# Order of the w_in column groups: attention's queries, keys and values first, retention's behind them

## The reference, cut to what matters

```python
h = rmsnorm(x, g_mix)
z = h @ w_in
aq, ak, av, rq, rk, rv, rg, ga, gb = jnp.split(z, SPLIT_POINTS, axis=-1)
aq = rope_half(aq.reshape(B, S, N_Q_HEADS, HEAD_DIM), pos)
ak = rope_half(ak.reshape(B, S, N_KV_HEADS, HEAD_DIM), pos)
ya = sliding_window_sink_attention(aq, ak, av, sinks) @ w_a
rq = retention_rotation(rq.reshape(B, S, RET_HEADS, RET_QK_DIM), pos)
rk = retention_rotation(rk.reshape(B, S, RET_HEADS, RET_QK_DIM), pos) * (RET_QK_DIM ** -0.5)
r = chunkwise_retention(rq, rk, rv)
r = r * lax.rsqrt(jnp.mean(r * r, axis=-1, keepdims=True) + EPS)
yb = (r.reshape(B, S, RET_V) * jax.nn.silu(rg)) @ w_b
x = x + (jax.nn.sigmoid(ga) * ya + jax.nn.sigmoid(gb) * yb) @ w_out
x = x + jnp.square(jax.nn.relu(rmsnorm(x, g_mlp) @ w_up)) @ w_down
```

## Time and profile before

| | before |
|---|---|
| runs shown | 1014.49, 1015.31, 1015.38 us, median 1015.31 us |
| the profiled execution | 1015.0 us, its span 1013.1 us |
| mean granted TensorE clock in it | 0.998 |
| busy: PE, DVE, ACT, POOL | 99%, 71%, 50%, 17% of the span |
| DMA, mean | 186 GB/s, 188.60 MB |

### The profile page before, as it was taken

The page is one execution under the profiler, slowest core; times in us unless marked ns, Lnnn a source line. Parts: engine busy times, 40 slices in busy tenths (PEclk is TensorE's granted clock), DMA queues, the critical chain, the costliest instruction groups (busy, mean ns, idle before and its releaser), DMA issues.

```text
span 1013.1 us, 13575 instructions
## 1 busy us (share of the span) xinstructions
PE 1004.5 (99%) x5653; PEld 850.0 (84%) x5653; DVE 720.8 (71%) x817; ACT 502.3 (50%) x616; POOL 170.7 (17%) x129
## 2 busy tenths in 40 slices
PE   9999999999999999999999999999999999999997
PEld 8887788888888888887788888888887899899796
DVE  5878656766565665787765667888877757789974
ACT  6544554454444545454554454444468545654352
POOL 0520000000000000430000020000000149169730
PEclk9999999999999999999999999999999999999999
DMA  9797444555556455596553557555554754345451
GB/s 341 250 288 246 160 155 142 170 180 191 199 176 207 166 178 175 187 294 225 166 167 125 169 147 283 201 177 209 204 170 135 238 178 167 125 166 141 121 188 41
DMA packets 103644, 188.60 MB, mean 186 GB/s; under 512 B 9160, under 2 KB 18464, under 8 KB 103456
## 3 DMA queue, kind: packets, MB, share of 16 engines
q1 hardware_dynamic: 103408, 187.66, 55.8%
q10 hardware_dynamic: 176, 0.09, 0.0%
HBM read 180.69 MB, written 4.72 MB: 183 GB/s over the span
## 4 chain that ended last, share of the span: by engine, by line
PE 93%; DVE 3%; DMA 1%; issue 1%; ACT 1%; SPq 0%; DVEq 0%; ACTq 0%
PE bank L786 13%; PE bank L789 12%; PE bank L788 12%; PE bank L1091 11%; PE bank L811 8%; PE bank L815 7%; PE bank L822 7%; PE bank L1095 6%; PE bank L1173 2%; DVE w_lo L1873 2%; PE bank L984 1%; PE bank L1397 1%; PE bank L968 1%; DMA a_bounce<-arena 1%; PE bank L793 1%; PE bank L803 1%
## 5 line engine op out<-in xcount | busy, mean ns | idle before, releaser
L1873 DVE TENSOR_TENSOR w_lo<-arena,w_hi 128x2048 fp32r<-128x2048 f32 (+1 forms) x80 | 185.1, 2323 | 95.2 <-ACT w_hi L1485 94.8
L1873 DVE TENSOR_TENSOR w_lo<-raw,w_hi 128x2048 fp32r<-128x2048 f32 (+1 forms) x78 | 181.1, 2331 | 80.1 <-ACT w_hi L1485 80.0
L1485 ACT ACTIVATE w_hi<-raw 128x2048 fp32r<-128x2048 f32 (+1 forms) x83 | 157.1, 1892 | 102.3 <-PE bank L789 71.4
L1485 ACT ACTIVATE w_hi<-arena 128x2048 fp32r<-128x2048 f32 (+1 forms) x80 | 151.3, 1892 | 104.6 <-PE bank L789 80.8
L1091 PE MATMUL bank<-hT,w_hi 128*128 128x512 f32 x504 | 123.4, 391 | 0.0
L786 PE MATMUL bank<-w_hi,hT 128*128 128x512 f32 (+1 forms) x296 | 114.1, 385 | 0.9 <-issue 0.9
L1091 PEld LDWEIGHTS bank<-hT,w_hi 128*128 128x128 f32 x504 | 92.2, 188 | 17.6
L2482 POOL TENSOR_TENSOR rstd<-mean,const 128x1 f32<-128x1 f32 (+1 forms) x16 | 9.1, 579 | 528.5 <-DVE mean L1882 359.4
L789 PE MATMUL bank<-w_hi,hT 128*128 128x512 f32 (+1 forms) x256 | 97.9, 382 | 0.0
L788 PE MATMUL bank<-w_lo,hT 128*128 128x512 f32 (+1 forms) x256 | 97.9, 382 | 0.0
L811 PE MATMUL bank<-w_hi,hT 128*128 128x512 f32 (+1 forms) x216 | 83.3, 388 | 0.7 <-DVE arena L2131 0.7
(11 more groups left out here) (342 smaller groups left out, 1886.7 us busy)
## 6 DMA issues: line engine op xcount, KB each, us to landing
arena<-in_w_in SPq DMA_DIRECT2D x22, 1024.0 KB, 5.3
raw<-in_w_in SPq DMA_DIRECT2D x20, 1024.0 KB, 5.3
arena<-in_w_up SPq DMA_DIRECT2D x16, 1024.0 KB, 5.3
raw<-in_w_up SPq DMA_DIRECT2D x16, 1024.0 KB, 5.3
arena<-in_w_down SPq DMA_DIRECT2D x16, 1024.0 KB, 5.1
raw<-in_w_down SPq DMA_DIRECT2D x16, 1024.0 KB, 5.1
raw<-in_e_w_in SPq DMA_DIRECT2D x6, 1024.0 KB, 5.1
arena<-in_e_w_in SPq DMA_DIRECT2D x6, 1024.0 KB, 5.1
```

The lines of the kernel that those rows point to most:

```text
L1485: act.activation(w_hi[:, p % SPLIT_RING, :, 0:n], raw_at(p)[:, :, 0:n], copy).then_inc(hi_ready, 1)
L1873: dve.tensor_tensor(w_lo[:, s, :, 0:n], raw_at(p)[:, :, 0:n], w_hi[:, s, :, 0:n].bitcast(F32), ALU.subtract).then_inc(lo_ready, 1)
```

## The change

The groups are numbered `AQ, AKV, RQ, RK, RV0, ...`. What depends on the numbers moves with them:

- the first group is AQ, the second the 256 columns of AKV, so that `second_group` is half as wide as before
- the tables att_cos and att_sin (64 KB) are loaded by themselves ahead of piece 3, the others ahead of piece 4 as before
- DVE runs `rotate_halves` in the window of g = 1 and `rotate_pairs` in that of g = 3, both with lo splits between; POOL runs them in that order too
- `turn_vectors` stands one group later on PE, and `spread_dt` on DVE behind the whole of `rotate_halves`
- SP stores attention's rows at piece 10 in one DMA (before: two, at 14 and 15) and fetches them at piece 11 in four (before eight, at 15); retention's rows are stored at 13 and fetched at 15 (before 12 and 13)
- DVE transposes aT at the start of g = 4 and rT at that of g = 6, each ahead of the next lo split (before rT at 5, aT at 6)
- attention's scores and softmax stand in the windows 4 to 7 (before 6 to 9), the transposes of probabilities in 5 to 8, the products with the values in 6 to 9 (bank 4, before 3); retention's scores in 6, 7 and 8 through bank 3 alone, its output in 8 and 9 (before 10 and 11 and behind), in the banks 6/7 and 2/5. No step stands behind the last group any more
- the second bank pair of the product with w_a waits for retention's output (`r_ready`), and DVE waits for `vec_ready` only ahead of the MLP

The core of the diff:

```diff
-RQ, RK, AQ, AKV, RV0, RV1, RG0, RG1, GA0, GA1, GB0, GB1 = range(12)
-W_IN_START = (768, 1280, 0, 512, 1792, 2304, 2816, 3328, 3840, 4352, 4864, 5376)
+AQ, AKV, RQ, RK, RV0, RV1, RG0, RG1, GA0, GA1, GB0, GB1 = range(12)
+W_IN_START = (0, 512, 768, 1280, 1792, 2304, 2816, 3328, 3840, 4352, 4864, 5376)
...
             def load(piece):
+                if n[0] == 3:
+                    sp.dma_start(const[:, FIRST_TABLES:SECOND_TABLES], consts[:, FIRST_TABLES:SECOND_TABLES]).then_inc(att_tables, 16)
...
             def blocks_moved(l, piece):
-                if piece == 12:
+                if piece == 10:
+                    for t in range(T):
+                        sp.wait_ge(rope_done[t], l + 1)
+                    store_rows(a_bounce.rearrange("(t p) n -> p t n", p=P), a_rows, a_stored)
+                if piece == 11:
+                    sp.wait_ge(a_stored, 16 * (l + 1))
+                    fetch_blocks(a_moved, a_bounce, a_blocks)
+                if piece == 13:
                     for t in range(T):
                         sp.wait_ge(rot_done[t], l + 1)
                     store_rows(r_bounce.rearrange("(t p) n -> p t n", p=P), z_ret, r_stored)
-                if piece == 13:
+                if piece == 15:
                     sp.wait_ge(r_stored, 16 * (l + 1))
                     fetch_blocks(r_moved, r_bounce, r_blocks)
...
@@ PE, in the stream of w_in @@
             def window(l, g):
-                if l == 0 and g == 1:
+                if l == 0 and g == 2:
                     turn_vectors()
...
-                if 6 <= g < 6 + PAIRS:
-                    i = g - 6
+                if 4 <= g < 4 + PAIRS:
+                    i = g - 4
...
-                if 7 <= g < 7 + PAIRS:
-                    n = l * PAIRS + g - 7
+                if 5 <= g < 5 + PAIRS:
+                    n = l * PAIRS + g - 5
                     pe.wait_ge(probs_ready, n + 1)
...
@@ DVE, in the stream of w_in @@
             def window(l, g):
                 if g == 1:
-                    dve.wait_ge(const_landed, 16)
-                    dve.wait_ge(sink_landed, 16)
-                    dve.wait_ge(vec_ready, 3)
-                    rotate_pairs(dve, order, l, 0, z_ga, between=lambda part: step(l * PIECES + 2 * AQ + 1 + part))
+                    dve.wait_ge(att_tables, 16)
+                    rotate_halves(dve, order, l, 0, z_ga, between=lambda part: step(l * PIECES + 5 + part))
                 if g == 3:
-                    rotate_halves(dve, order, l, 0, z_ga)
+                    dve.wait_ge(const_landed, 16)
+                    rotate_pairs(dve, order, l, 0, z_ga, between=lambda part: step(l * PIECES + 8 + part))
...
-                if 6 <= g < 6 + PAIRS:
-                    softmax(l, g - 6)
-                if g == 10:
-                    retention_out(l, 0)
+                if 4 <= g < 4 + PAIRS:
+                    softmax(l, g - 4)
+                if g in (8, 9):
+                    retention_out(l, g - 8)
...
                 for g in range(W_IN_GROUPS):
                     if g == 4:
-                        window(l, g - 1)
+                        dve.wait_ge(a_blocks, 16 * BLOCKS * (l + 1))
+                        turn_blocks(aT, a_moved, A_SLOTS).then_inc(aT_ready, 1)
+                        dve.wait_ge(aT_ready, l + 1)
                     if g == 6:
-                        dve.wait_ge(a_blocks, 16 * T * BLOCKS * (l + 1))
-                        turn_blocks(aT, a_moved, A_SLOTS).then_inc(aT_ready, 1)
-                    if g == 5:
                         dve.wait_ge(r_blocks, 16 * BLOCKS * (l + 1))
                         turn_blocks(rT, r_moved, 2 * RET_HEADS).then_inc(rT_ready, 1)
-                    if g != AKV and (l or g):
+                    if g not in (3, 4) and (l or g):
                         step(p + 2 * g)
-                    if l == 0 and g == 1:
+                    window(l, g - 1)
+                    if l == 0 and g == 2:
                         spread_dt()
-                    if g != 4:
-                        window(l, g - 1)
-                    if g != AQ:
+                    if g not in (2, 4):
                         step(p + 2 * g + 1)
...
@@ POOL @@
             row_scale(0)
-            pool.wait_ge(const_landed, 16)
-            pool.wait_ge(vec_ready, 3)
+            pool.wait_ge(att_tables, 16)
             for l in range(DEPTH):
+                rotate_halves(pool, order, l, 1, z_gb)
+                if l == 0:
+                    pool.wait_ge(const_landed, 16)
+                    pool.wait_ge(vec_ready, 3)
                 rotate_pairs(pool, order, l, 1, z_gb)
-                rotate_halves(pool, order, l, 1, z_gb)
```

More of the change, by code:

```diff
@@ L155, in shape_constants @@
     at, where = 0, {}
-    order = list(KEPT_TABLES) + [n for n in tabs if n not in KEPT_TABLES + LATE_TABLES] + list(LATE_TABLES)
+    known = KEPT_TABLES + ATT_TABLES + LATE_TABLES
+    order = list(KEPT_TABLES + ATT_TABLES) + [n for n in tabs if n not in known] + list(LATE_TABLES)
     for name in order:
@@ L180, in build_program @@
         FIRST_TABLES = where[KEPT_TABLES[-1]][1]
+        SECOND_TABLES = where[ATT_TABLES[-1]][1]
         raw = sb("raw", [P, RAW_KEPT, KP, COLS])
@@ L404, in build_program @@
         rT_ready = sem("rT_ready")
-        a_stored = [sem(f"a_stored{t}") for t in range(T)]
+        a_stored = sem("a_stored")
         a_blocks = sem("a_blocks")
@@ L587, in rotate_pairs, with rotate_halves @@
             eng.wait_ge(rot_done[t], l + 1)
-        def rotate_halves(eng, o, l, t, tmp):
+        def rotate_halves(eng, o, l, t, tmp, between=lambda part: None):
             for g in (AQ, AKV):
@@ L953, in second_group @@
             def second_group():
+                width = AKV_WIDTH
                 for i in range(2):
@@ L967, in second_group @@
                             for kk in range(KP):
-                                last = pe.matmul(OUT[t], a[:, i * KP + kk, at], w[:, s, kk, :],
+                                last = pe.matmul(OUT[t][:, 0:width], a[:, i * KP + kk, at], w[:, s, kk, 0:width],
                                                  start=(i == kk == 0 and w is w_hi and a is hT_hi),
@@ L1004, in window @@
             def window(l, g):
-                if l == 0 and g == 1:
+                if l == 0 and g == 2:
                     turn_vectors()
-                if g == 5:
-                    pe.wait_ge(rT_ready, l + 1)
+                if g == 4:
+                    pe.wait_ge(aT_ready, l + 1)
                     if l == 0:
                         pe.wait_ge(vec_ready, 3)
-                    for n in range(T):
-                        at = slice(n * P, (n + 1) * P)
-                        for hd in range(RET_HEADS):
-                            last = pe.matmul(bank[:, 3 + n, hd * P:(hd + 1) * P], rkT[:, hd, at], rqT[:, hd, at],
-                                             start=True, stop=True)
-                        last.then_inc(s_ret_done, 1)
-                if g == 6:
-                    pe.wait_ge(s_ret_ready, 2 * l + 1)
+                if g in (6, 7):
+                    n = g - 6
+                    if n == 0:
+                        pe.wait_ge(rT_ready, l + 1)
+                    else:
+                        pe.wait_ge(s_ret_ready, 2 * l + 1)
+                    at = slice(n * P, (n + 1) * P)
+                    for hd in range(RET_HEADS):
+                        last = pe.matmul(bank[:, 3, hd * P:(hd + 1) * P], rkT[:, hd, at], rqT[:, hd, at], start=True, stop=True)
+                    last.then_inc(s_ret_done, 1)
+                if g == 8:
+                    pe.wait_ge(s_ret_ready, 2 * l + 2)
                     for hd in range(RET_HEADS):
@@ L1646, in _ @@
                     window(l, g - 1)
[L1647 removed]
+                    if g != AQ:
                         step(p + 2 * g + 1)
                     group_out(l, g)
[L1650 removed]
                 step(p + PIECE_A)
@@ L2157, in _ @@
                         dve.tensor_tensor(x[:, t, at], OUT[t], x[:, t, at], ALU.add).then_inc(out_free[t], 1)
+                dve.wait_ge(vec_ready, 3)
                 turn_lo(4 * l + 3, gain=V_MLP + KD * l)
```

102 lines of the change are left out of this document (44 added, 58 removed).

## The result

| | before | after |
|---|---|---|
| median of the runs | 1015.08 us (4 runs) | 1050.51 us (4 runs, 1046.24 to 1052.06) |
| ratio | | 1.0343, 95% interval 1.0311 to 1.0375 |
| profiled execution | 1015.0, span 1013.1 | 1051.5, span 1049.6 |
| mean granted clock | 0.998 | 0.983 |

A forecast was written before the change was run, and what follows sets the result against it. TensorE was taken as the bound, busy 1004.5 of 1013.1 us, so the price is its new waits. 2.5 + 7.9 + 2.0 + 6.4 + 6.8 + 7.3 - 1.6 = 31.3, added to 1015.3, gave 1046.5 us; range 1028 to 1055.

The forecast's parts named there:

- Term 1: Layer 0, start of RQ: PE waits for ACT to evacuate AKV behind piece 5's hi split, +2.5 us.
- Term 2: Layer 0, after RQ: PE waits for DVE's copy of dt, now behind all of rotate_halves, +7.9 us.
- Term 3: Layer 0, after the stop for dt: PE's clock falls to 1.2 GHz, +2.0 us (0 to 2.8).
- The rival of the clock falling: Clock also drops at three waits of 4.2 to 4.3 us in both layers: 5.6 us more, 1052, chance 0.12.
- Term 4: Layer 0, windows 5 and 6: retention's round trip delays the softmax, PE waits at probabilities and banks, +6.4 us.
- Terms 5 and 6: Layer 1: attention's round trip makes PE wait, +6.8 us, and retention's round trip, +7.3 us.
- Term 7: PE's two named idle times, 0.7 us at the gated retention group and 0.9 us elsewhere, vanish: -1.6 us.
- The first rival: Both layers: retention's trips land in time, so stops of 6.4 and 7.3 us vanish: 1033, chance 0.15.

The follow-up runs named there:

- experiment 1: Changed kernel with dt laid out by DVE one group earlier, before its rotation: 1040.43 us against 1050.5.
- experiment 4: Changed kernel with 26 matmuls of 128x128 into an unused bank ahead of PE's wait for the dt copy: 1045.87 us against 1050.5.
- experiment 5: Changed kernel with DVE's wait for retention's fetched rows, and their transpose, moved behind the softmax of pair 1: 1037.29 us against 1050.5.
- (8): Changed kernel with DVE's softmax of pair 0 ahead of the lo split of piece 12: 1049.17 us against 1050.5.
- (9): Changed kernel with dt early, AKV evacuated first, retention's fetch behind one load, its wait behind softmax 1, softmax 0 earlier: 1023.88 us; reordered further: 1016.45, then 1014.41.

## Why the prediction was right, and where its terms were off

The direction, the places of the stops and, within the range, the sum held; the split between waits and clock didn't. That the sum came so near is partly luck: the waits were forecast some 5 us too long, the clock some 10 too short. By its own terms:

- **Term 1** (2.5): the wait is there, by ACT's order, and measured 4.2 in the profiled run (3.1 to 3.7 in the profiles of six other versions that have it). The mis-sized part is when piece 5 lands. I took the transfers as limited by bandwidth at 391 GB/s throughout, so 1.05 MB less meant 2.7 us earlier. The chain of waits shows its load released by DVE's lo split that frees the slot, at 15.72, and landing 11.94 us later, only 0.4 earlier than before:

```profile
14.58 1.14 DVE w_lo L1931
...
15.74 11.94 DMA raw<-in_w_in
...
29.52 0.47 ACT arena L1504
```

That lo split begins at 14.50 us, 0.9 later than before (13.60), and in 12 to 16 us the transfers moved 246 GB/s instead of 386. How the two share the lost 2.3 us isn't shown.

- **Term 2** (7.9): 6.3, at the place and by the chain that was forecast; experiment 1 confirms it. The rest of the rotation behind the lo split took 1.3 us (47.65 to 48.98), not the 2.9 of the earlier trace rows: POOL's rotation used to run beside it and now ends at 42.6.
- **Term 3** (2.0) is the one that failed. As the price of one stop it was right: 2.4 by experiment 4. But I charged it once, and the clock fell behind every group of stops in w_in, in five stretches with 12.2 us lost. The forecast put four of them at nothing, and its reason against the rival, that PE is fully busy right before and after each wait, didn't hold. The rival of the clock falling "at the three long waits too" was nearer to the truth, and I had given it 0.12; even it left out the stop at RQ and took 1.9 us for each, where the stretch behind layer 0's window 6 alone lost 3.8 (half of 7.6). Even layer 1's stop of 1.9 us, which ends at 484.57, is followed by 0.50 from 485.1 to 488.4.
- **Term 4** (6.4): the stops in layer 0's windows 5 and 6 are 8.7 us (4.2 at the probabilities in two waits, 2.3 at the scores, 1.9 for rT, 0.3 at the banks). The trip took 20.1 instead of 16.5. By the forecast the turned rows are there 2.4 us before PE has ended RG0 (90.7 and 93.1); they came 1.9 after it. The rest of the mechanism, the lo split and the softmax behind DVE's wait, is shown by experiment 5.
- **Terms 5 and 6** (6.8 and 7.3): 6.3 in sum, 6.0 of it at the probabilities. Attention's trip took 11.5 us, as taken (11.3), and retention's 16.8 (16.5). But rotate_pairs ended at 476.3, 4.4 us earlier than reckoned (49.3 behind AKV's start at 431.3): attention's rows were there 1.2 earlier, since that rotation too had ended earlier, and the two multiplies between the lo splits took 0.68 us each, not 2.0. The timelines of DVE and POOL, layer 0 and layer 1:

```profile
69.41 2.02 DVE L583 TENSOR_TENSOR arena<-arena,const 128x512 f32<-128x512 f32 x1
...
67.30 3.58 POOL L583 TENSOR_TENSOR arena<-arena,const 128x512 f32<-128x512 f32 x1
...
471.55 0.68 DVE L583 TENSOR_TENSOR arena<-arena,const 128x512 f32<-128x512 f32 x1
...
462.25 1.50 POOL L583 TENSOR_TENSOR arena<-arena,const 128x512 f32<-128x512 f32 x1
...
466.80 1.53 POOL L590 TENSOR_TENSOR arena<-arena 128x512 f32<-128x512 f32 x1
```

In layer 0 both engines work at the same time and a multiply of 128x512 takes DVE 2.0 us and POOL up to 3.6; in layer 1 POOL was done at 468.3, before DVE began its own at 471.55, and they take 0.68 and 1.5. I had carried the duration of the earlier trace rows over, which was measured beside a busy POOL.

- **Term 7** (-1.6): half right. The 0.9 us at L786 are gone (L792 shows none), the 0.7 at the banks of the gated group stand as before, now given to ACT's hi split.
- **Two slips in the sums.** In term 4, 93.1 + 0.9 + 0.4 + 0.9 is 95.3, not 95.0, so the wait was 4.0 by its own terms; and the forecast's own range begins at 1040, not 1039. Neither bears on the result.

So some 24 us of waits, where 29 were forecast net of term 7 and without the clock, and 12 of clock, where 2 were. The first rival, that retention's trips land in time, is out: the trips were as long as in the rows of before or longer, and with it falls the estimate of 8.8 us by the Trainium skill's fit for the GpSimd path ("DMA: Bandwidth & Descriptors", the section on the anatomy of one DMA); 13.5 us is the shortest of retention's trips measured above.

## What to carry to other kernels

Where an engine works in order, moving a wait forward moves everything behind it: look for what stands behind each wait on a transfer, and put the wait where its data is due and not where it is first possible. Price each stop of TensorE with its clock: here a stop of 6 us cost 2.4 more. The price of a single stop is only a start: six of the seven single edits paid 4.6 to 13.2 us here, but one edit of a chain can be given back at the next link (8), and one that paid (5) became the bound once another had shortened what it waited for (9).

## What the runs showed of the hardware that was not expected

A load of 1.05 MB less ahead of a fetch in the same queue shortened the round trip by 5.1 and 3.3 us, not by the 2.7 that 391 GB/s gives. A DVE multiply of 128x512 took three times as long beside a busy POOL (2.02 against 0.68 us), and one of POOL's more than twice as long beside a busy DVE (3.58 against 1.50). And a stop of only 1.9 us in PE was followed by the 1.2 GHz level: PE resumed at 484.57 and had a granted clock of 0.50 from 485.1 to 488.4, while the stop of 0.8 us at 87 us alone was followed by none. Behind the stop of 4.2 us, too, the clock fell only after PE had resumed, at 31.1 against 30.12.
